# A decoder step with expert retrieval: activations laid as 64 tokens by two column halves, and expert layers that take half of the tokens through all heads, then the rest

## The reference, cut to what matters

```python
q = (x2 @ w_q).reshape(T, PEER_HEADS, 2, PEER_HALF)                # 8 heads, 2 x 128
s = jnp.einsum('thpd,hpnd->thpn', q, sub_keys)                     # 128 keys a side
sv, si = lax.top_k(s, PEER_TOPK)                                   # 16 a side
cand = (sv[:, :, 0, :, None] + sv[:, :, 1, None, :]).reshape(T, PEER_HEADS, 256)
top_s, top_i = lax.top_k(cand, PEER_TOPK)                          # 16 of 256 experts
gate = jax.nn.softmax(top_s, axis=-1)
h = jnp.einsum('td,ted->te', xb, u_tab[ib])                        # ib: 8 x 16 experts a token
act = jax.nn.gelu(h, approximate=False) * gb
out = jnp.einsum('te,ted->td', act, v_tab[ib])
```

## Time and profile before

| | us |
|---|---|
| time, median of 3 runs | 4109.46 (4107.18 to 4110.72) |
| profiled execution, span of its one core | 4109.2 |
| PE busy | 3515.8 (86%) |
| DVE busy | 2578.8 (63%) |
| ACT busy | 1476.6 (36%) |
| POOL busy | 1346.6 (33%) |
| HBM read, written | 1197.88 MB, 7.86 MB |
| the gathers' queue | 1133.58 MB, 67.6% of 16 DMA engines over the span |

### The profile page before, as it was taken

The page is one execution under the profiler, slowest core; times in us unless marked ns, Lnnn a source line. Parts: engine busy times, 40 slices in busy tenths (PEclk is TensorE's granted clock), DMA queues, the critical chain, the costliest instruction groups (busy, mean ns, idle before and its releaser), DMA issues. The chain is left out here.

```text
span 4109.2 us, 48131 instructions
## 1 busy us (share of the span) xinstructions
PE 3515.8 (86%) x13271; PEld 1898.3 (46%) x13271; DVE 2578.8 (63%) x6388; ACT 1476.6 (36%) x4181; POOL 1346.6 (33%) x1196
## 2 busy tenths in 40 slices
PE   7997888888888797888789789899888888888887
PEld 6877785434333343333344467654333333333332
DVE  3665443777777777777734434347767677676775
ACT  2451111334343433434412332124433434443442
POOL 0004330343444444444500011014444444434442
PEclk9997889999999999999989899899999999999998
DMA  2220002899999999999950035449999999999998
GB/s 94 72 73 20 12 12 108 351 415 405 410 408 402 411 405 407 407 402 408 421 204 7 11 119 208 160 165 417 418 405 408 404 414 402 411 401 411 406 413 333
DMA packets 193619, 1208.34 MB, mean 294 GB/s; under 512 B 28872, under 2 KB 40400, under 8 KB 56800
## 3 DMA queue, kind: packets, MB, share of 16 engines
q0 software_dynamic: 153600, 1133.58, 67.6%
q1 hardware_dynamic: 39776, 72.24, 5.1%
HBM read 1197.88 MB, written 7.86 MB: 293 GB/s over the span
## 5 line engine op out<-in xcount | busy, mean ns | idle before, releaser
L1280 PE MATMUL po<-ring,diag 128*128 128x512 f32 x4096 | 2001.4, 636 | 396.8 <-ACT diag L1065 394.7
L1013 POOL DMA_INDIRECT ring<-in_uv,idx x1024 | 1163.7, 1136 | 1741.2 <-PE po L1280 1354.8
L1142 DVE SCALAR_TENSOR_TENSOR ring<-ring,xn 128x1024 f32<-128x1024 f32 x1024 | 1225.2, 1223 | 595.8 <-DMA ring<-in_uv,idx 541.1
L1280 PEld LDWEIGHTS po<-ring,diag 128*128 128x128 f32 x4096 | 782.8, 201 | 1424.5 <-issue 769.8
L1059 ACT ACTIVATE hg<-hs 128x1 f32<-128x1 f32 x1024 | 203.5, 199 | 1338.5 <-DVE ring L1142 1332.3
L1065 ACT ACTIVATE diag<-const,hgg 128x128 f32<-128x128 f32 x1024 | 411.3, 402 | 59.8
L1061 ACT ACTIVATE hgg<-hg,gate 128x1 f32<-128x1 f32 x1024 | 302.0, 295 | 47.9 <-issue 10.1
L1197 PE MATMUL wide<-xnT,w 128*128 128x512 f32 (+1 forms) x512 | 255.3, 584 | 0.0
L292 PE MATMUL acc<-xnT,w 128*128 128x260 f32 x1024 | 230.2, 386 | 0.7 <-ACT inp L413 0.7
L292 PEld LDWEIGHTS acc<-xnT,w 128*128 128x128 f32 x1024 | 196.1, 192 | 38.0 <-issue 7.2
L1198 PEld LDWEIGHTS wide<-xnT,w 128*128 128x128 f32 x512 | 98.3, 192 | 110.4 <-issue 108.5
(11 more groups left out here) (482 smaller groups left out, 3978.9 us busy)
## 6 DMA issues: line engine op xcount, KB each, us to landing
w<-in_w_gdn SPq DMA_DIRECT2D x32, 512.0 KB, 3.5
w<-in_w_peer SPq DMA_DIRECT2D x32, 512.0 KB, 8.5
ring<-in_uv,idx POOLq DMA_INDIRECT x1024, 12.0
out_ssm_s<-states SPq DMA_DIRECT2D x4, 1024.0 KB, 5.1
ring<-in_w_gdn_out SPq DMA_DIRECT2D x8, 512.0 KB, 6.1
ring<-in_w_mla_out SPq DMA_DIRECT2D x8, 512.0 KB, 6.8
wq<-in_w_uq SPq DMA_DIRECT2D x1, 3072.0 KB, 21.0
x<-in_x_prompt SPq DMA_DIRECT2D x1, 2048.0 KB
```

What stands on the lines that cost most here:

```text
L1013: pool.indirect_dma_start(out=ring[:, c % RING, :], out_offset=None, in_=uv, in_offset=bass.IndirectOffsetOnAxis(ap=idx[t % 2][:, c:c + 1] ...
L1142: dve.scalar_tensor_tensor(ring[:, c % RING, 0:D], ring[:, c % RING, 0:D], 1.0, xn[:, t, :], ALU.mult, ALU.mult, accum_out=hs[a][:, c:c + ...
L1280: last = pe.matmul(po[a][:, HALF * e:HALF * e + HALF], diag[:, c % RING, :], ring[:, c % RING, D + HALF * e:D + HALF * e + HALF], start=c ...
```

## The change

`core.x` now lies as 9 groups of 64 tokens (the ninth holds the 8 samples and zeros). A group is 128 partitions by 512 columns: partitions 0 to 63 hold the left half of the columns, 64 to 127 the right half. A norm needs a sum over both halves: a matmul with the constant C_PAIR makes it. `norm` goes through nine groups, is used in both layers, and stands ahead of `mla_in` as a block of its own.

`peer` takes half of the prompt (256 tokens, two tiles) through all 8 heads, then the other half with the samples' queries: 32 units, u = 2hh + tile, with hh from 0 to 15. A gather brings two slots of 64 tokens: partitions 0 to 63 take one expert of each of 64 tokens, partitions 64 to 127 another expert of the same tokens; the first eight gathers of a unit serve its first group, the rest its second. PE lays the indices and the gates out for that (`lay`), DVE makes the index an integer (`place`), ACT copies the gates. The token rows are repeated for both slots (`repeat`, buffer `rep`). ACT's diagonal has 64 columns, and PE's two matmuls a slot are 64 wide, into partitions 0 to 63 and 64 to 127 of one bank. The projection is done in such pieces too, and so is the samples' last product, in two pieces in place of four. `w_out` has its own buffer. The second half's projection, norm and turning lie in units 1 to 3 and 13. SP loads a query weight block and its keys for each half; the samples' top-k runs once, for all heads, in the last unit. The hardware loop is gone.

```diff
-WEIGH_C = 8
+WEIGH_C = 6
...
-LATE_QUERIES = {0: (0, 0), 1: (0, 2), 2: (0, 4), 3: (0, 6), 5: (1, 0), 6: (1, 2), 7: (1, 4), 8: (1, 6)}
+HEADS = 2 * H
+UNITS = 2 * HEADS
+HALF_ROWS = SEQ // 2
+LATE = ((16, (4, 5)), (30, (6, 7)), (44, (8,)))
+LATE_TURN = (13, {1: 4, 3: 5, 5: 6, 7: 7, 9: 8})
+SAMPLE_C = 6
...
+        wo = core.sbuf(ctx, "wo", [P, KD, D])
+        rep = core.sbuf(ctx, "rep", [P, 4, D])
         ring = core.sbuf(ctx, "ring", [P, RING, 2 * D])
-        wo = ring[:, RING // 2:, :].rearrange("p r n -> p (r n)").rearrange("p (k n) -> p k n", k=KD)
-        diag = core.sbuf(ctx, "diag", [P, RING, P])
+        diag = core.sbuf(ctx, "diag", [P, RING, TG])
...
-                for k in range(KD):
-                    sp.dma_start(wo[:, k, :], wd[:, k, :]).then_inc(s[f"o_w{k}"], 16)
-                sp.dma_start(gain, core.i["norm_ffn"][layer:layer + 1, :].to_broadcast([P, D])).then_inc(s["gain"], 16)
+                for i in range(4):
+                    sp.dma_start(wo[:, 2 * i:2 * i + 2, :], wd[:, 2 * i:2 * i + 2, :]).then_inc(s[f"o_w{i}"], 16)
+                def load(hh, p):
+                    h = hh % H
+                    sp.dma_start(w[:, p, :, :], weight[2 * h + p]).then_inc(s[f"w{p}"], 16)
+                    sp.dma_start(sk[:, hh % 2, p, :], keys[:, 2 * h + p, :]).then_inc(s[f"w{p}"], 16)
+
                 for p in range(2):
-                    sp.dma_start(w[:, p, :, :], weight[p]).then_inc(s[f"w{p}"], 16)
-                sp.dma_start(sk[:, :, :], keys).then_inc(s["inp"], 16)
+                    load(0, p)
-                with sp.Fori(1, H) as h:
+                for hh in range(1, HEADS):
                     for p in range(2):
-                        after(sp, at("q_made", h - 1, p + 1))
-                        sp.dma_start(w[:, p, :, :], weight[ds(2 * h + p, 1), :, :, :].rearrange("o p k n -> (o p) k n")).then_inc(s[f"w{p}"], 16)
+                        after(sp, (s["q_first"], 4) if hh == 1 else at("q_made", hh - 2, p + 1))
+                        load(hh, p)
...
-                        apart(pool, at("top", u, TOP_STEPS))
-                        for c in range(TOPK):
-                            if first and t == 0 and c == RING // 2:
-                                pool.wait_ge(s["o_made"], 2 * T)
-                            if c >= RING or t or not first:
-                                apart(pool, at("pv", u, c - RING + 1))
-                            pool.indirect_dma_start(out=ring[:, c % RING, :], out_offset=None, in_=uv,
-                                                    in_offset=bass.IndirectOffsetOnAxis(ap=idx[t % 2][:, c:c + 1], axis=0)).then_inc(s[f"landed{c % RING}"], 16)
-
+                for u in range(UNITS):
+                    after(pool, at("placed", u, 1))
+                    for c in range(TOPK):
+                        if u or c >= RING:
+                            after(pool, at("pv", u, c - RING + 1))
+                        pool.indirect_dma_start(out=ring[:, c % RING, :], out_offset=None, in_=uv,
+                                                in_offset=bass.IndirectOffsetOnAxis(ap=idx[u % 2][:, c:c + 1], axis=0)).then_inc(s[f"landed{c % RING}"], 16)
...
-                            act.activation(diag[:, c % RING, :], core.ident, ACT.Copy, scale=hgg[a][:, c:c + 1]).then_inc(s["diag"], 1)
...
+                        act.activation(diag[:, c % RING, :], core.const[:, C_PAIR, 0:TG], ACT.Copy, scale=hgg[a][:, c:c + 1]).then_inc(s["diag"], 1)
...
+                def place(v):
+
+                    after(dve, at("mixed", v, 1))
+                    dve.tensor_scalar(idx[v % 2][:, :], pR[:, 0, :], 0.25, None, ALU.add).then_inc(s["placed"], 1)
...
+                    dve.tensor_scalar(gate[:, :], k.e[:, :], k.z[:, 1:2], None, ALU.mult).then_inc(s["gate"], 1)
+
+                def add(u, i):
+
+                    g = 2 * tile_of(u) + i
+                    after(dve, at("pv", u, RING * i + RING))
+                    dve.tensor_tensor(core.x[:, g, :], acc[i][:, :], core.x[:, g, :], ALU.add).then_inc(s["added"], 1)
...
+                        if u < UNITS - 1:
+                            if c == 1:
+                                retrieve(u + 1, 0)
+                            if c == 4:
+                                retrieve(u + 1, 1)
+                            if c == 7:
+                                place(u + 1)
+                            if c == 8:
+                                weighed(u + 1)
+                        if c == 9:
+                            add(u, 0)
+                        if c == 2 and u:
+                            add(u - 1, 1)
+                        for d, groups in late(n):
...
-                            if c == 3 and more:
-                                retrieve(u + 1, 1 - a, 0)
-                            if c == 7 and more:
-                                retrieve(u + 1, 1 - a, 1)
-                            if c == 11:
-                                if t or not first:
-                                    add(u - 1, (t - 1) % NT)
-                                if more:
-                                    weighed(u + 1, 1 - a)
-                            if (t, c) == ((1, 5) if first else (0, 13)):
-                                apart(dve, at("sscored", h, 1), at("sexped", h, 0))
-                                top_k(dve, s, "stop", h, ks, pT, counting, part(sidx, h, TOPK), 0)
-                            if c == 13 and t == 1:
-                                top_k(dve, s, "stop", h, ks, pT, counting, part(sidx, h, TOPK), 1)
...
+                            for j in range(2):
+                                last = pe.matmul(summed(g)[rows(j), :], lhs, wo[:, kk, column(j)], start=kk == 0, stop=kk == KD - 1)
...
+                def score(v):
+
+                    hh, t = v // 2, v % 2
+                    after(pe, (s["first_out"], 2 * t + 2) if hh == 0 else at("q_out", hh - 1, 2), at("top", v, 0))
+                    if hh > H:
+                        after(pe, at("scopied", hh - H - 1, 1))
+                    for p in range(2):
+                        last = pe.matmul(pS[:, p, :], q[:, p, P * t:P * t + P], sk[:, hh % 2, p, :], start=True, stop=True)
...
+                def lay(v, e, src):
+
+                    after(pe, at("placed", v, e), at("gated", v, 0))
+                    for i in range(2):
+                        for r in range(2):
+                            last = pe.matmul(pR[rows(r), e, RING * i:RING * i + RING], core.const[:, C_ID, rows(i)], src[:, RING * r:RING * r + RING], start=True, stop=True)
+                    last.then_inc(s["mixed"], 1)
...
+                for u in range(UNITS):
+                    a, hh = u % 2, u // 2 + 1
+                    for c in range(TOPK):
+                        n, r, i = TOPK * u + c, c % RING, c // RING
+                        after(pe, at("diag", u, c + 1))
+                        if r == 0:
+                            after(pe, at("added", u - 1, i + 1) if u else (s["o_added"], 4))
+                        for j in range(2):
+                            last = pe.matmul(acc[i][rows(j), :], diag[:, r, :], ring[:, r, D + HALF * j:D + HALF * j + HALF], start=r == 0, stop=r == RING - 1)
+                        last.then_inc(s["pv"], 1)
+                                score(u + 1)
+                                after(pe, at("top", u + 1, TOP_STEPS))
+                                lay(u + 1, 0, index)
+                            if c == 9:
+                                after(pe, at("gate", u + 1, 2))
+                                lay(u + 1, 1, gate)
...
+                        if a == 0 and hh < HEADS:
+                            if 4 <= c < 8:
+                                queries(hh, 0, 2 * c - 8, 2 * c - 6)
+                            if 9 <= c < 13:
+                                queries(hh, 1, 2 * c - 18, 2 * c - 16)
+                        for d, groups in late(n):
+                            if d < KD:
+                                project(groups, d, d + 1)
...
-                                last = pe.matmul(po[a][:, HALF * e:HALF * e + HALF], diag[:, c % RING, :], ring[:, c % RING, D + HALF * e:D + HALF * e + HALF],
-                                                 start=c == 0, stop=c == TOPK - 1)
...
-                sp.dma_start(gain, core.i["norm_mix"][1:2, :].to_broadcast([P, D])).then_inc(s["n_gain"], 16)
-                wd = core.i["w_mla_in"].rearrange("(k p) n -> p k n", p=P)
-                sp.dma_start(w[:, :, 0:QL], wd[:, :, 0:QL]).then_inc(s["w_q"], 16)
-                sp.dma_start(w[:, :, QL:], wd[:, :, QL:]).then_inc(s["w_k"], 16)
...
-                            last.then_inc(s["n_turned"], 1)
-
-                turn(0)
-                turn(1)
...
+                    def ask(sp):
+                        wd = core.i["w_mla_in"].rearrange("(k p) n -> p k n", p=P)
+                        sp.dma_start(w_in[:, :, 0:QL], wd[:, :, 0:QL]).then_inc(come["w_in_q"], 16)
```

(4 more changed lines are left out.)

847 lines of the change are left out of this document (448 added, 399 removed).

## The result

The changed kernel takes 4069.6 us (median of 4 runs, 4060.5 to 4072.0) against 4109.1 for the kernel before (4107.2 to 4110.7): a ratio of 0.9903 (95% interval 0.9889 to 0.9917), 40 us faster. The forecast was 4044, in a range of 4014 to 4100. The sign and the range held. The gain is 61% of the one forecast, and its parts are not the forecast ones. The profiled execution is the fastest of the four: 4060.5, with a span of 4058.7. So in the profiles 50.5 us are to be accounted for, out of 65 forecast.

The account below looks back on a forecast made before the run. DMA bytes in the two gather stretches bound the kernel. Per layer: stretch -27, lead-in -18, tail +4, so -41; two layers -82; norms +7 and +8, loads and stores +2: -65 from 4109.2, so 4044 us, range 4014 to 4100.

Parts of the forecast that it names:

- Matmuls of half width overlap: PE in the gather stretches: a slot's two 64-wide matmuls run together, 0.86 us a slot in place of 1.72.
- rival 3: PE's half-width matmuls do not overlap, a slot stays at 1.72 us: +95 a layer, 4234 us; chance 4%.
- So the dry spells should go: 2.49 us per gather: Gather stretches: DMA engines no longer run dry behind retrievals; 2.49 us per gather, bounds 2.48 and 2.57.
- rival 1: Gather stretches: half of the engines' dry time stays, 2.53 us per gather, +40: 4084 us; chance 14%.
- The walk through a unit from "caught-up": One unit's gathers: issued ones keep engines busy until 30 us, slot free at 21; margin 2 to 4 us.
- The second DVE block as the trigger: Gather stretches before: the samples' top-k blocks DVE again before it has caught up, and the engines run dry.
- rival 2: Dry spells stay whole, as POOL's wait is not for PE's speed: 2.57 us per gather, 4124 us; chance 6%.
- 3 for the projection and norm of the second half: Units 1 to 3: this late work on PE and DVE adds 3 us to a layer's gather stretch.
- Weights and keys twice: Per layer, 30 query weight loads at 1.26 us (37.8) and 30 key transfers at 0.25 us (7.5) while gathers run.
- Lead-in: First w_out DMA to first gather: 47.7 us against 65.3, -18 a layer; then eight gathers go at once.
- Tail: After a layer's last gathers: final products +5, four copies gone -2, idx later +1, so +4 a layer.
- Norms: Nine groups in place of five tiles, 23 us against 15.5: +7; attention's norm as separate block, 26 us: +8.

Follow-up runs that it names:

- after: The changed kernel itself in its profiled execution, the fastest of four: 4060.5 us (median of the runs 4069.6).
- doubled products: Changed kernel with the two 64-wide products of a slot done twice in 6 slots of 8: 4113.6 us, ratio to before 1.0012.
- the run with 8 rows: Changed kernel in which PE repeats a sample's row by a product over 8 rows of the array, not 128: 4072.2 us.

## Why the prediction was right, and where not

- **What bounds the kernel**: right. Bytes in the gather stretches set the time. The runs without the second weights and with short keys moved it by about what those bytes take.
- **Matmuls of half width overlap**: right, and rival 3 (4%) falls. In after:

```profile
2038.03 2.87 PE L1422 MATMUL acc<-ring,diag 128*64 128x512 f32 x12
```

Twelve records in 2.87 us; in series, at 0.43 each, they would take 5.2.

- **"So the dry spells should go: 2.49 us per gather"**: this step failed. Of 43 us a layer, 19 stay. Without the weights (38 us by the forecast's price) and the keys (30 at the 0.19 measured, 6), the stretch of layer 0 is 1287 us: (1287 - 5.4 - 4.5) / 503 = 2.54 us per gather, layer 1 2.55; less the forecast's 3 us for the late work, 2.53 and 2.54. The forecast had called itself wrong above 2.53. In size it is rival 1, *the dry spells half stay*, to which I gave 14%. In the forecast the gather stretches miss by 19.5 and 25.7 us. The walk through a unit from "caught-up" is right for a unit without query steps: POOL's gap of 6.92 us costs nothing there, and the ordinary units of this kind lose 1.3 us in one layer and nothing in the other. It left out the units with query steps, in which a step of 1.1 to 2.1 us stands behind each product of the backlog: 12.4 us a layer. Taking the retrieval out of these units nearly filled the rate there; thinning out or moving the steps did not, so what in them makes the spells is not settled. The prediction itself had named the query matmuls as the third feeder of the spells, and the walk then priced only the second block.
- **The second DVE block as the trigger**: in part. Left out of the kernel before, it gives 10 us. PE's slow products, put back into the changed kernel, cost 44, but nearly all of it in units that also carry the late projection or the change of halves; in the ordinary units they add 4 us a layer. That the wait is not one for PE's speed, which rival 2 says, is nearly so in these units, though the spells did not stay whole. Of rival 1's reasons the DVE block counts (half of the blocks, 9 us), moving the two table loads gained nothing, and the new wait in place is 1.04 us.
- **"3 for the projection and norm of the second half"**: not measured by itself, but this is where PE has the least room: with doubled products units 0 to 3 grew by 15.9 and 13.8 us, units 15 and 16 by 12.3 and 10.0.
- **Weights and keys twice**: right, 1.18 us a load for 1.26 taken, 0.19 for 0.25.
- **Lead-in**: right to 2 us, -17.5 and -16.4 for -18. The first gather comes 47.8 us after the first w_out DMA; the sum said 47.7. DVE's retrieval in it ran as in the earlier trace rows, and after it the eight gathers went out in a row:

```profile
646.05 2.20 SPq L1014 DMA_DIRECT2D wo<-in_w_gdn_out  x4
...
650.94 15.31 PE L1314 MATMUL big<-wo,oT 128*64 128x512 f32 x64 [8.02 <-DMA wo<-in_w_gdn_out]
...
682.86 0.50 DVE L874 MAX8 sv<-pS 128x8 f32<-128x128 f32 x2 [7.52 <-PE pS L1375]
...
693.86 1.11 POOL L1048 DMA_INDIRECT ring<-in_uv,idx  x1 [92.55 <-DVE idx L1191]
```

- **Place and lay**: no trouble. DVE waits 1.04 us for `lay` at `place` (27.1 us in 26 units of the window), inside the 1 to 1.5 forecast.
- **Tail**: wrong in sign, -4.9 and -6.1 for +4. In layer 0 the parts are: the last products +3.7 (5.09 us before, 8.78 after; 7.09 in layer 1), where +5 was foreseen; the copies and sums behind them -2.3, where -2 was; the first sample's product comes 2.2 us sooner behind the last gather, where +1 was; and -4.1 for the pace of the eight samples, at which I did not look. Before, the last four samples came 3.42 us apart: DVE waited 2.18 us for PE's repeated row, which took 3.61 us at the lower clock. After, a row takes 1.98 us and the samples come 2.5 us apart, the pace at which the gathers land. Before and after:

```profile
2082.84 3.61 PE L1204 MATMUL po<-xns,const 8*128 8x512 f32 x4
2083.07 1.22 DVE L1174 SCALAR_TENSOR_TENSOR ring<-ring,wide 128x1024 f32<-128x1024 f32 x1 [2.18 <-PE wide L1204]
```

```profile
2051.35 1.98 PE L1389 MATMUL big<-xns,const 128*128 128x512 f32 x4 [0.51 <-DVE ring L1290]
2052.56 1.22 DVE L1290 SCALAR_TENSOR_TENSOR ring<-ring,big 128x1024 f32<-128x1024 f32 x1 [1.27 <-DMA ring<-in_uv,sidxT]
```

That the rows of after run at the higher clock is read from them; why, the run with 8 rows could not tell. It had three of its last four rows at the lower clock, and its samples still came every 2.5 us, since its rows are short. Both tails give 19 us against the forecast and hide nearly half of the miss in the stretches.

- **Norms**: right in size. The first gated delta weight DMA comes at 37.2 us in after and at 29.1 before, +8.1 for +7. The block behind it happened to be some 6 us shorter in this execution: in the eleven runs of changed variants the first w_out DMA comes at 651.2 to 652.6, not at 646.05. That is most of the 9 us by which the profiled execution lies under the median. The attention's norm takes 25.0 us (26 forecast), and the attention's page table is asked for 188.9 us after its beginning, before 182.2: +6.7 for +8. The rest of the attention was 5.6 us shorter, and it varies: the attention took 550.4 to 555.8 us in all in the runs with doubled products, few query steps, no second weights and short keys.

In one line: -65 forecast, +45 from the gather stretches, +2 from the lead-ins, -19 from the tails, -14 from the stages with the norms and their chance differences: -50.5, the profiled execution's gain. The chances had rival 1 at 14% with 4084. Its size came true in the stretches, and the tails, which no rival spoke of, together with blocks of the norm stages that happened to be short, brought the time back between it and the forecast. That it came so near the forecast is luck: errors of +47 and -33 us met. The range would have held without it: 4044 and 47 are 4091, below 4100.

## What to carry to other kernels

When a full queue runs dry, find out in which units it does before naming a cause. An average over the stretch fitted "PE's speed" here; by units the slow products cost some 40 of their 48 us in six units of a layer where PE had other work, and the spells that were left lay in the units that have a long DVE block and query steps together. Moving the query steps only moved the spells here, so look for a unit with room before you move work. Price a repeated load by its bytes at the stretch's own rate, and take it off the gain before anything else; here the bytes added (29 us) ate all that the shallower spells had won in the stretch (24 us), and most of the gain left is the shorter lead-in, with eight gathers ready behind it. In a tail, work out the pace of each engine per item, at the clock that the rows show there.
